# Splitting the first four weight quarters of a layer before the layer begins: twelve layers of a transformer on one core

## The reference

```python
for i in range(DEPTH):                       # DEPTH = 2
    h = rwkv7_time_mix(x, ...) if i % 2 == 0 else moba_attention(x, ...)
    x = layer_norm(ALPHA * x + h, ln_mix_g[i], ln_mix_b[i])
    x = layer_norm(ALPHA * x + swiglu_ffn(x, ffn_w_in[i], ffn_w_down[i]), ln_ffn_g[i], ln_ffn_b[i])
...
for i in range(DEPTH_2):                     # DEPTH_2 = 4: conv, near, hyena, conv
    h = rmsnorm(x, norm_mix_g[i])
    ...
    x = x + y
    x = x + swiglu(rmsnorm(x, norm_ffn_g[i]), f_w13[i], f_w2[i])
```

## Time and profile before

| | |
|---|---|
| device time, median of 3 runs | 2058.32 us (2056.6 to 2060.03) |
| span of the profiled execution | 2053.3 us |
| PE busy | 1994.9 us (97%) |
| DVE busy | 1277.7 us (62%) |
| ACT busy | 909.9 us (44%) |
| POOL busy | 161.9 us (8%) |
| chain that ended last | PE 87%, DVE 8%, issue 2% |

### The profile page before, as it was taken

How to read it: one execution, slowest core, us unless ns; L and a number is a source line. 1 busy time by engine, 2 the same in 40 slices (tenths; PEclk the granted TensorE clock), 3 DMA queues, 4 the chain that set the end, 5 groups by cost and what they waited for, 6 DMA issues and landing times.

```text
span 2053.3 us, 32584 instructions
## 1 busy us (share of the span) xinstructions
PE 1994.9 (97%) x12754; PEld 1615.8 (79%) x12754; DVE 1277.7 (62%) x1623; ACT 909.9 (44%) x1282; POOL 161.9 (8%) x198
## 2 busy tenths in 40 slices
PE   7999999999999999999999999999999999999999
PEld 6689688878678879888878678877767888897887
DVE  7784755477665556655757655576985554575553
ACT  4462344434444434444545454434434444444442
POOL 2152100000010010000002011001100000000000
PEclk9999999999999999999999999999998999999999
DMA  8321365555166655465555257553324555555554
GB/s 302 113 70 38 102 211 184 185 172 179 61 205 204 195 174 172 167 209 188 167 185 192 71 169 224 192 185 133 103 73 132 190 184 187 171 169 185 185 167 150
DMA packets 93040, 335.95 MB, mean 164 GB/s; under 512 B 11230, under 2 KB 11364, under 8 KB 92623
## 3 DMA queue, kind: packets, MB, share of 16 engines
q1 hardware_dynamic: 85824, 311.62, 45.9%
q0 software_dynamic: 7120, 22.95, 4.0%
HBM read 332.43 MB, written 1.05 MB: 162 GB/s over the span
## 4 chain that ended last, share of the span: by engine, by line
PE 87%; DVE 8%; issue 2%; ACT 1%; POOL 1%; DMA 0%; SPq 0%; DVEq 0%; ACTq 0%; POOLq 0%
PE acc L361 42%; PE acc L448 20%; PE acc L419 9%; DVE w_lo L1554 2%; PE acc L920 2%; PE aux L841 1%; PE aux L468 1%; PE aux L625 1%; PE aux L876 1%; POOL rstd L2371 1%; PE aux L908 1%; DVE operand_lo L1575 1%; ACT w_hi L1169 1%; PE acc L612 1%; PE aux L897 1%
## 5 line engine op out<-in xcount | busy, mean ns | idle before, releaser
L1554 DVE TENSOR_TENSOR w_lo<-w_raw,w_hi 128x1024 fp32r<-128x1024 f32 x588 | 717.3, 1225 | 575.1 <-ACT w_hi L1169 570.4
L1169 ACT ACTIVATE w_hi<-w_raw 128x1024 fp32r<-128x1024 f32 x588 | 620.9, 1060 | 792.9 <-PE acc L361 447.9
L361 PE MATMUL acc<-w_hi,operand_hi 128*128 128x512 f32 x1344 | 535.5, 398 | 26.9 <-DVE operand_lo L1720 12.1
L361 PE MATMUL acc<-w_hi,operand_lo 128*128 128x512 f32 x1344 | 526.4, 392 | 0.0
L361 PE MATMUL acc<-w_lo,operand_hi 128*128 128x512 f32 x1344 | 525.9, 391 | 0.0
L361 PEld LDWEIGHTS acc<-w_hi,operand_hi 128*128 128x128 f32 x1344 | 253.7, 189 | 91.3 <-DVE operand_lo L1575 15.3
L361 PEld LDWEIGHTS acc<-w_hi,operand_lo 128*128 128x128 f32 x1344 | 253.2, 188 | 53.5
L361 PEld LDWEIGHTS acc<-w_lo,operand_hi 128*128 128x128 f32 x1344 | 253.9, 189 | 50.3 <-issue 0.5
L448 PE MATMUL acc<-w_hi,hidden_hi 128*128 128x512 f32 x528 | 210.3, 398 | 0.0
L448 PE MATMUL acc<-w_hi,hidden_lo 128*128 128x512 f32 x528 | 208.5, 395 | 0.0
L448 PE MATMUL acc<-w_lo,hidden_hi 128*128 128x512 f32 x528 | 208.4, 395 | 0.0
(11 more groups left out here) (474 smaller groups left out, 2117.2 us busy)
## 6 DMA issues: line engine op xcount, KB each, us to landing
w_raw<-in_weights SPq DMA_DIRECT2D x588, 512.0 KB, 3.4
ln_gain<-in_gains POOLq DMA_DIRECT2D x7, 512.0 KB, 5.0
bias_at<-in_rpb POOLq DMA_DIRECT2D x12, 256.0 KB, 5.5
ln_gain<-in_ln_g POOLq DMA_DIRECT2D x4, 512.0 KB, 4.1
ln_bias<-in_ln_b POOLq DMA_DIRECT2D x4, 512.0 KB, 5.4
vec_rw<-in_vec POOLq DMA_DIRECT2D x3, 512.0 KB, 5.9
l_rw<-in_lora SPq DMA_DIRECT2D x1, 1152.0 KB, 10.4
iclr_rw<-in_xT SPq DMA_DIRECT2D x2, 512.0 KB, 4.5
```

Source lines behind the costliest of these rows:

```text
L361: mm = pe.matmul(acc[:, 2 * pair + t, :], (ah, al)[x][:, kt, t * P:(t + 1) * P], W[w][:, s, kk * 512:(kk + 1) * 512], start=(kt == 0 and ( ...
L1169: act.activation(whi[:, s, :], raw[:, s, :], ACT.Copy).then_inc(w_hi[s], 1)
L1554: dve.tensor_tensor(wlo[:, s, :], raw[:, s, :], whi[:, s, :].bitcast(F32), ALU.subtract).then_inc(w_lo[s], 1)
```

## The change

Nine of the eleven layers behind the first (`spared`: all but near and hyena) get a second place for their first four quarters, the tile `w_spare`, 2 x 4 quarters. It lies in memory that the other layers don't use at that time; near's tile for the high part of its bias is now a view of it, and two RWKV tiles are laid down in another order to fit. Since no one waits for these slots, ACT and DVE split the first three quarters of the next layer right behind the last quarter of the old one, before the passage, and the fourth inside it. In the two attention layers the first two of them stand in the tail of the last head pairs and the third at the start of the passage. PE reads `weight(x, q)`, which is the spare place or the ring. The splits that were in the passages are gone from them, and `add`, `operand` and the fourth split have a new order on DVE. `keep_busy` is gone from `first_block`'s quarters. The quarters behind the first four find the ring already free. POOL's first loads for hyena wait for at least the fourth quarter.

```diff
+        SPARE = attend("w_spare", [P, 2, SLOTS, QW], F32R)
...
+    BIASH = SPARE[:].rearrange("p x s n -> p (x s n)")[:, 0:HEADS * BIAS_W].rearrange("p (h n) -> p h n", h=HEADS)
...
+    spared = [n for n, kind in enumerate(layers) if n and kind not in ("near", "hyena")]
+    beside_ring = {start[n] + i: i for n in spared for i in range(SLOTS)}
+    def weight(x, q):
+        return SPARE[:, x, beside_ring[q], :] if q in beside_ring else W[x][:, q % SLOTS, :]
...
@@ first_block (PE)
                     if t == 0:
-                        if src is X:
-                            keep_busy((0, 0, 3, 1)[i])
                         pe.wait_ge(w_lo[(q + i) % SLOTS], nth(q + i))
...
@@ split (ACT)
-            if q >= SLOTS:
-                act.wait_ge(w_used[s], nth(q - SLOTS, at))
-            act.activation(whi[:, s, :], raw[:, s, :], ACT.Copy).then_inc(w_hi[s], 1)
+            if q >= SLOTS and q not in beside_ring:
+                act.wait_ge(w_used[s], nth(q - (2 if q - SLOTS in beside_ring else 1) * SLOTS, at))
+            act.activation(weight(0, q), raw[:, s, :], ACT.Copy).then_inc(w_hi[s], 1)
...
@@ residual (ACT)
+            if early and kind in ("moba", "near"):
+                ahead(q - 2, 1)
+            if early and channels:
+                square(0)
+                ahead(q - 1, 1)
+                square(1)
+                both_operands()
+                return
+            if early:
+                if rms:
+                    square(0)
+                operand(0)
+                ahead(q - 1, 1)
+                if rms:
+                    square(1)
+                operand(1)
+                return
...
@@ rwkv, conv, hyena (ACT and DVE)
-            ahead(q + IN_Q, OUT_Q - 4)
+            ahead(q + IN_Q, OUT_Q - 1)
...
@@ ffn (ACT and DVE)
-                for k in range(FK - 4):
+                for k in range(FK - 4 if following == "hyena" else FK - 1):
...
@@ attention (ACT and DVE)
-                if 2 <= p <= OUT_Q - 3:
+                if p >= 2:
                     split(q + IN_Q + p - 2 + SLOTS)
...
@@ residual (DVE)
+            if early and kind in ("moba", "near"):
+                ahead(q - 2, 1)
+            if early and layer_norm:
+                add_with_stats(0, 0)
+                add_with_stats(0, 1)
+                moments(0)
+                centred(0)
+                normed(0)
+                add_with_stats(1, 0)
+                if not rms:
+                    operand(0)
+                add_with_stats(1, 1)
+                moments(1)
+                centred(1)
+                ahead(q - 1, 1)
+                normed(1)
...
+            if early:
+                add(0, 0)
+                add(0, 1)
+                rms_normed(0)
+                if channels:
+                    add(1, 0)
+                    add(1, 1)
+                    ahead(q - 1, 1)
+                    rms_normed(1)
+                    both_operands()
+                else:
+                    operand(0, (0,))
+                    add(1, 0)
+                    operand(0, (1,))
+                    add(1, 1)
+                    ahead(q - 1, 1)
+                    rms_normed(1)
+                    operand(1)
+                return
```

More of the change, by code:

```diff
@@ L151, in program @@
         RBT = rwkv("rb_rw", [P, TT, 2, KT, CH])
+        [FM] = scope(("transition_rw", [P, 2, KT, HD]))
+        KTT = rwkv("k_turned", [P, KT, SEQ])
         CUM, SPAN = scope(("cum_rw", [P, 2, P]), ("span_rw", [P, TT, 3]))
@@ L154, in program @@
         BTT = rwkv("b_turned", [P, KT, SEQ])
-        [FM] = scope(("transition_rw", [P, 2, KT, HD]))
-        KTT = rwkv("k_turned", [P, KT, SEQ])
         G2 = rwkv("g2_rw", [P, D])
@@ L355, in part_tokens @@
         def part_tokens(q, i, pair, t, beside=None):
-            s = (q + i) % SLOTS
             for kk in range(2):
@@ L361, in part_tokens @@
                     mm = pe.matmul(acc[:, 2 * pair + t, :], (ah, al)[x][:, kt, t * P:(t + 1) * P],
-                                   W[w][:, s, kk * 512:(kk + 1) * 512],
+                                   weight(w, q + i)[:, kk * 512:(kk + 1) * 512],
                                    start=(kt == 0 and (x, w) == (0, 0)), stop=(kt == KT - 1 and (x, w) == (1, 0)))
@@ L419, in block_channels @@
                             mm = pe.matmul(acc[:, 2 * pair + c // 2, (c % 2) * SEQ:(c % 2 + 1) * SEQ],
-                                           W[w][:, s, kk * 512 + c * P:kk * 512 + (c + 1) * P], (ah, al)[x][:, kt, :],
+                                           weight(w, q + i)[:, kk * 512 + c * P:kk * 512 + (c + 1) * P], (ah, al)[x][:, kt, :],
                                            start=(kt == 0 and c % 2 == 0 and (x, w) == (0, 0)),
@@ L1194, in residual @@
             channels = more and layers[n + 1] in ("conv", "hyena")
+            early = n + 1 in spared
             def square(t):
@@ L1553, in split @@
             dve.wait_ge(w_hi[s], nth(q, at))
-            dve.tensor_tensor(wlo[:, s, :], raw[:, s, :], whi[:, s, :].bitcast(F32), ALU.subtract).then_inc(w_lo[s], 1)
+            dve.tensor_tensor(weight(1, q), raw[:, s, :], weight(0, q).bitcast(F32), ALU.subtract).then_inc(w_lo[s], 1)
         def ahead(q, n, at=None):
@@ L2507, in load_next @@
                 slow[0] += 1
-                pool.wait_ge(w_used[(q + 3 * k // 2) % SLOTS], nth(q + 3 * k // 2))
+                used = q + max(SLOTS - 1, 3 * k // 2)
+                pool.wait_ge(w_used[used % SLOTS], nth(used))
                 load(dst, src, m["hyena_in"])
```

1 line of the change is left out of this document (removed).

## The result

The changed kernel takes 2063.92 us in the median (2060.15 to 2069.09, 17 runs), the kernel before 2057.41 (2052.72 to 2062.34, 17 runs). The ratio is 1.0034, 95% interval 1.0025 to 1.0042: slower by 0.34%, about 6.5 us. That is inside the range, on the side to which I gave 0.26, and the time of the rival "the clock falls in the passages" (2063.5).

The account below looks back on a forecast made before the run. It took PE to bound the kernel, with waits only in the passages and mixers. Span 2053.3 less 2.35 gained in passages plus 2.5 lost to the clock, plus 5.0 to the median, gave 2058.5 us; range 2049.5 to 2065.

Parts of the forecast that it names:

- the clock falls in the passages: Rival: PE's clock falls in five or six passages at 1.4 us each, giving 2063.5 us; chance 0.22.
- the slow rival: The rival that PE's clock falls in five or six passages, 2063.5 us; chance 0.22.
- Three splits move ahead of the first add: In DVE's queue before the passages: first add 2.3 us later behind a FFN, 3.6 behind RWKV.
- The passages' sum: Gains and losses of the nine changed passages, before any clock loss, add to 2.35 us gained.
- POOL beside the fourth split: DVE's fourth split delays POOL's work on tile 1's squares: 0.3 us in each of six RMS chains.
- The clock: New idle times of PE before tile 0's turn lower its granted clock: 2.5 us lost, bounds 0 and 10.2.
- my sign of being wrong: Wrong if the first add isn't later, or if PE's long idle times leave the clock at 1.00.
- From span to median: The median of the runs lies 5.0 us over the profiled span, so 2053.45 becomes 2058.5.
- The place and the layout at nothing: The memory's new layout and the earlier splits of the quarters behind the first four cost or gain nothing.
- The gain behind moba: Passage from moba: two splits ahead hide in the mixer's tail, PE's tile 1 comes 2.5 us earlier.
- free: Rival: the splits ahead end before the first add, each passage some 1.7 us shorter, 2043 us; chance 0.05.
- never early: Rival: the quarters ahead lack raw data, so all four splits still fall into the passages, 2062 us; chance 0.04.

Follow-up runs that it names:

- e4: The kernel before with the spare place and new order only in the passage from moba to ffn: 2054.65 us, ratio 0.9981.
- e7: The kernel before with two filling matmuls on PE ahead of the first turn after RWKV: 2059.47 us beside 2061.74.
- e1: The changed kernel's place and layout, but the numbers of splits ahead, DVE order and fillers of the kernel before: 2058.05 us, ratio 0.9997.
- e2: The changed kernel with filling matmuls on PE ahead of the first turn behind RWKV, first ffn to moba, convs and hyena: 2060.71 us, ratio 1.001.
- e3: The changed kernel with two quarters instead of three split ahead of the sums after RWKV, ffn, conv and hyena: 2059.03 us, ratio 1.0004.
- e6: The changed kernel with the four splits spread over DVE's waits, plus fillers before turns after RWKV, before moba, after conv and hyena: 2045.88 us, ratio 0.9933.

## Why the prediction was right and wrong

The number was 2058.5; 2063.92 was measured, inside the range and 5.4 us beside the number. I had forecast a time level with before, and it is 6.5 us slower. The range held because it reached to the slow rival, not because the sum was right. By its steps:

*Three splits move ahead of the first add.* The direction was right and the size wrong. Behind RWKV I had them end near 233.1, behind the convs and hyena 3.4 to 3.8 us late. Measured, the first adds are 5.1 us later (RWKV, first conv), 5.6 (hyena), 5.2 (last conv) and 2.8 behind the FFN (2.3 in the prediction). I took 4.3 us as the landing time of a quarter from four transfers that nobody waited for, and 1.17 as the distance of the splits; I left out that the transfers follow one another through busy DMA engines, so every quarter ahead arrives 2.2 to 2.6 us after the one before it. Part of this stood in the trace of the kernel before: there the same four quarters, issued 1.34 to 1.36 us apart from 224.43 on, land at 227.67, 230.12, 231.37 and 233.75. With the third at 231.37 its two splits would end at 233.7, not 233.1. The rest is that in the changed kernel the third took 5.19 us to land instead of 4.24, with a fifth transfer under way.

*The passages' sum.* I had 2.35 us gained. ffn to conv (+1.53 and +0.47 measured, +1.6 and +0.3 predicted) was right, near to ffn (+0.06 against +0.6) nearly so. moba to ffn gained 1.17 against 2.5, and e4, with its 2.16, points to the fall inside the mixer as the difference, worth 1.4 in e7 and e1. With the clock held in e2, RWKV, ffn to moba, conv, hyena and last conv come to +1.21, -0.30, +0.53, -0.21 and +0.69, together 1.9 lost where I had 2.35 gained: 4.3 us too good in this trace. By the runs (3.8 us left for the waits against 2.35 gained) the term was some 6 us too good. This is the step that carries the miss. What it left out is the wait for the data of the second and third split; e3, with the third moved back, gets 3.2 of the 3.8 again.

*POOL beside the fourth split.* I had counted 0.3 us in each of six chains, and the trace of the changed kernel doesn't show it where the fourth split stands in a passage into a FFN. Behind the conv, DVE's split and POOL:

```profile
876.92 1.22 DVE L1577 TENSOR_TENSOR w_spare<-w_raw,w_spare 128x1024 fp32r<-128x1024 f32 x1
```
```profile
876.57 0.19 POOL L2449 TENSOR_SCALAR stat<-stat 128x1 f32<-128x1 f32 x1 [4.65 <-ACT token_scratch L1209]
877.94 0.34 POOL L2452 TENSOR_SCALAR stat<-stat 128x1 f32<-128x1 f32 x1 [1.17 <-ACT token_scratch L1209]
```

One operation ends before the split starts and the other starts near its end. The same holds behind near, hyena and the last conv: neither operation takes over 0.35 us. Longer ones stand in ffn to conv: in the first (0.65 to 1.22, against 0.61 to 0.75 before) and one in the second (0.93, against 0.20). In e3, with two splits at this place, they take 0.57 and 1.10 behind the conv.

*The clock.* I had 2.5 us, from two long idle times at 0.9 and 2/7 of four short ones. By the runs' clocks it is 2.8, so the size of the whole term is right, but in part by luck, since the falls came elsewhere. I had RWKV's passage and the first ffn to conv fall and the last two hold. RWKV's fell; ffn to conv held, with an idle time of 3.47 us, so for this one my sign of being wrong came true; and behind hyena and the last conv a new wait took the place of the old one and the clock fell. The idle times are longer, since the splits are later (4.92 for 3.4 behind RWKV; 2.9 to 3.5 behind the convs and hyena, where I had named only hyena's, at 1.7 to 1.9). The rival named its own point, more than three passages with a clock under 1: there are five in this trace. The price of 0.9 for a fall of 1.7 was about right on average: 1.0 by the fit, 1.1 over the four of e7. e2's five passages got more back, 9.2 us for 11.9 us of clock, from 1.46 where 3.42 had been lost to 2.38 where 1.70 had; over 1.7 for one fall can't be the clock alone.

*From span to median.* I added 5.0 us. The later runs list both, and each takes 1.7 to 1.9 us more than its own span; the other 3.2 were there because the profiled execution was shorter than most (mean clock 0.995 against 0.9936). The changed kernel's was longer than most (0.990 against 0.9913), which is part of why the spans lie 11.4 apart.

*What held.* The place and the layout at nothing, within the caution at e1. The first add held by DVE's own splits. The gain behind moba, where two splits hide in the mixer's tail. The rivals "free" and "never early" are out: of the three quarters ahead, all are early for PE, and all are late for DVE.

*What stays open.* The medians differ by 6.5 us and the table's sum by 12.1, and I have one trace of each kernel. The 2.8 and 3.8 us rest on a fit over runs and could each be off by some 0.7. Which waits bring a fall in an execution, and what part the missing `keep_busy` has in ffn to moba, no run here shows.

## What to carry to other kernels

Work that is off the critical engine's path must still not stand in an in-order queue ahead of the one instruction for which that engine waits: with three of four splits ahead of the first add the kernel lost 6.5 us (the clock included), with the four laid one by one into DVE's own waits it gained 18.7. When work is pulled ahead, price its input as well: if it was paced by buffers that come free late, it will be paced by their transfers now. And fill PE's wait only where the trace shows one; the two or three fillers in a queue without a wait cost 1.5 to 1.7 us a passage (e6), more than the 1.0 of an average fall. Where the runs list their mean clock, use it: it parts a fall from a wait better than one trace of each kernel.

## What the runs showed of the hardware

Every fall of TensorE's clock inside the layers took 1.70 us of clock or twice or three times that (1.64 to 1.72, 3.42, 5.12). By the Trainium skill, "TensorE: Matmul & The Clock Gate", section "HAM oscillation — how this bites in real kernels", it is long idle gaps that bring the clock down. The traces bear that out only loosely: waits of 1.72 and 1.83 us brought falls (e7), one of 3.47 didn't in the changed kernel, and one of 3.48 did in e2. So what a wait of this size costs can't be told from its length. A single fall was worth 0.5 to 1.8 us of a passage in e7, and 1.0 us of the whole time on average over the runs; executions of one program differ in mean clock by 0.006 (the kernel before), some 7 us of time by the fit.
